# First block of a three-block network: gate and attention output as seven products, with weight sums made by accumulating transfers

## The reference, cut to what matters

```
proj = x @ w_in                       # q, k, v, z_attn, z_ssm, xbc, dt
attn = sliding_window_attention(q, k, v, sinks) * silu(z_attn)
xs, B, C = split(silu(causal_depthwise_conv(xbc)))
y    = ssd_chunked(xs, dt, a, B, C) + xs * d_skip    # 2 chunks of 128, 2 groups of 8 heads
ssm  = gated_rmsnorm(y, z_ssm, ssm_norm_w)           # y * silu(z_ssm), normed per group of 512
out  = concat([attn, ssm]) @ w_out                   # w_out is 2048 x 1024
x    = layer_norm(ALPHA * x + out)
```

## Time and profile before

| | us |
|---|---|
| median of 3 runs | 1921.62 (1921.53 to 1923.89) |
| the profiled execution, its own time | 1921.72 |
| its span | 1919.5 |
| PE busy in the span | 1561.8 (81%) |
| DVE, ACT busy | 681.4 (35%), 306.8 (16%) |

### The profile page before, as it was taken

One profiled execution on the slowest core, in us unless ns is written; L12 is line 12 of the kernel. 1 busy time (PEld: TensorE's weight loads), 2 busy tenths in 40 slices (PEclk: granted clock), 3 DMA queues, 4 the chain that ended last, 5 costly groups with the idle time before them and its releaser, 6 DMA issues.

```text
span 1919.5 us, 20479 instructions
## 1 busy us (share of the span) xinstructions
PE 1561.8 (81%) x8818; PEld 889.4 (46%) x8818; DVE 681.4 (35%) x1395; ACT 306.8 (16%) x806; POOL 16.2 (1%) x45
## 2 busy tenths in 40 slices
PE   9999999999999999675655666555666556899999
PEld 6675477744667845232221222212222122457886
DVE  3663456634486964212110111111111111144533
ACT  1343313442112102000000000000000000213220
POOL 0000000000000000000000000000000000000000
PEclk9999999999999999888887877878787778899999
DMA  9861376523253457999999999999999999954300
GB/s 378 282 174 67 118 271 214 154 102 140 97 175 132 176 220 294 434 431 430 432 431 431 428 432 429 433 429 432 428 432 429 432 430 430 374 186 175 125 8 22
DMA packets 88419, 558.58 MB, mean 291 GB/s; under 512 B 4608, under 2 KB 11552, under 8 KB 74240
## 3 DMA queue, kind: packets, MB, share of 16 engines
q1 hardware_dynamic: 86544, 548.81, 71.3%
...
...
## 4 chain that ended last, share of the span: by engine, by line
PE 58%; DMA 35%; DVE 4%; ACT 1%; issue 1%; POOL 0%; SPq 0%; DVEq 0%; ACTq 0%; POOLq 0%
PE bank L683 26%; DMA ring<-in_w 22%; DMA arena<-in_w 13%; PE bank L1181 8%; PE bank L710 7%; PE bank L692 6%; PE bank L1209 3%; PE bank L671 2%; PE bank L1494 1%; PE bank L885 1%; PE bank L821 1%; PE bank L801 1%; DVE arena L2437 0%; PE bank L1152 0%; PE bank L1232 0%
## 5 line engine op out<-in xcount | busy, mean ns | idle before, releaser
L1181 PE MATMUL bank<-ring,arena 128*32 128x512 f32 x1216 | 288.0, 734 | 148.3 <-DMA arena<-in_w 102.3
L1181 PE MATMUL bank<-arena 128*32 128x512 f32 x832 | 235.5, 733 | 110.6 <-DMA ring<-in_w 98.7
L683 PE MATMUL bank<-ring,arena 128*128 128x512 f32 (+3 forms) x744 | 302.2, 559 | 0.0
L683 PE MATMUL bank<-arena,ring 128*128 128x256 f32 (+1 forms) x1632 | 292.0, 337 | 0.5 <-DVE arena L3116 0.5
L683 PEld LDWEIGHTS bank<-arena,ring 128*128 128x128 f32 x1632 | 256.0, 191 | 31.5 <-issue 7.3
L683 PEld LDWEIGHTS bank<-ring,arena 128*128 128x128 f32 x744 | 138.7, 190 | 134.5 <-issue 123.2
L1181 PEld LDWEIGHTS bank<-ring,arena 128*32 128x32 f32 x1216 | 71.7, 131 | 266.9 <-issue 266.9
L1181 PEld LDWEIGHTS bank<-arena 128*32 128x32 f32 x832 | 57.3, 131 | 202.2 <-issue 202.0
L1209 PE MATMUL bank<-ring,arena 128*32 128x512 f32 x576 | 113.8, 637 | 24.7 <-DMA arena<-in_w 13.8
L710 PE MATMUL bank<-ring,arena 128*128 128x512 f32 (+1 forms) x320 | 127.2, 554 | 2.4 <-DMA ring<-in_w_vd 1.4
L692 PE MATMUL bank<-arena,ring 128*64 128x256 f32 x1024 | 112.6, 380 | 0.0
...
## 6 DMA issues: line engine op xcount, KB each, us to landing
...
ring<-in_w_in SPq DMA_DIRECT2D x40, 2048.0 KB, 8.5
ring<-in_w_mod SPq DMA_DIRECT2D x6, 2048.0 KB, 12.9
ring<-in_w_out SPq DMA_DIRECT2D x6, 2048.0 KB, 8.0
arena<-in_w SPq DMA_DIRECT2D x6, 2048.0 KB, 11.1
ring<-in_w SPq DMA_DIRECT2D x6, 2048.0 KB, 11.7
ring<-in_w_out SPq DMA_DIRECT2D x16, 512.0 KB, 9.6
```

Source lines behind the costliest of these rows:

```text
L683: i = te.matmul(ps, lhsT, rhs, start=n0 + k == 0, stop=n0 + k == n - 1)
L1181: m = te.matmul(ps[32 * j:32 * j + 32, :], LM.xg[:, f, 128 * k + 32 * j:128 * k + 32 * j + 32], vs[j][:, 512 * (k % 2):512 * (k % 2) + 512 ...
```

## The change

Each of the two products is computed by the scheme of Strassen and Winograd: the input is cut in halves of tokens and of channels, the weight in four quadrants, and seven products of 128 tokens x 512 channels x 512 columns (four matmuls each) take the place of eight. The sums that it needs are made in this way.

* Weights: a new input `w_quads` holds the quadrants; SP loads slots `(name, 0)` and `(name, 1)` and a third, `("T", name)`, 2 MB each, for "zs" and "oa". POOL then issues four transfers of 1 MB each that add into their destination (`accum_op=ALU.add`): 1 and 3 add a quadrant from memory, 2 adds one half of T to the other, 4 adds T to the second half of slot 0. So 4 needs 2 and 3 and that product 2 has read slot 0.
* Inputs: four sums of 128x512 on DVE (`layer_token_sums`), for "zs" within the convolution, for "oa" after product 6 of "zs".
* Results: a running sum in `L1.part`; its start is written by ACT, the rest by DVE; tanh now reads `L1.zs`.

In "zs" product 7 comes three turns after product 6, the two between being empty. "oa" goes to the residual `h` at once, and `out_ssm` begins its banks afresh. The gate quarter (1, 0) is made last, after product 7. The turns of ACT's `layer_ssm` are reordered: the squares of a head group come after the first decays of the next. `lng` and `lnb` are loaded at the end of a layer, since the four sums lie in their place. 2 MB slots are counted from 1 instead of 5.

```diff
-            turn, in_turn = [5], list(range(NR))
+            turn, in_turn = [1], list(range(NR))
...
-                for n in range(2):
-                    ns = slice(512 * n, 512 * n + 512)
-                    layer_load(("oa", ly, n), *[(lambda v, a=a, kp=kp: v[64 * a:64 * a + 64, 4 * kp:4 * kp + 4, :],
-                                                 wo[0:1024, ns].rearrange("(k a g d) n -> k a d g n", k=2, a=2, g=4)[kp, a])
-                                                for a in range(2) for kp in range(2)])
+                load_quadrants(("zs", ly, 0), 0, 0)
+                load_quadrants(("zs", ly, 1), 0, 2)
+                load_quadrants(("T", "zs", ly), 0, 2)
+                load_quadrants(("oa", ly, 0), 1, 0)
+                load_quadrants(("T", "oa", ly), 1, 2)
+                load_quadrants(("oa", ly, 1), 1, 2)
...
+            def layer_seven(name, ly, xT):
+
+                w0, w1, T = weights((name, ly, 0)), weights((name, ly, 1)), weights(("T", name, ly))
+                lo, hi = slice(0, 128), slice(128, 256)
+                S = L1.sums
+
+                def times(k, x, w):
+                    ps = fresh("P", name, ly, k, b=4 + ((k - 1) if name == "zs" else k + 6) % 4)
+                    product(ps[:, :], [(x[:, c, :], w[:, c, :]) for c in range(4)]).then_inc(*t.done("mm", "P", name, ly, k))
+                t.wait_ge(*at.of("w", (name, ly, 0)))
+                times(1, xT[:, 0:4, lo], w0[:, 0:4, :])
+                yield
+                times(2, xT[:, 4:8, lo], w0[:, 4:8, :])
+                yield
+                ready(("w", (name, ly, 1)), ("S", name, ly))
+                times(3, S[3], w1[:, 4:8, :])
+                yield
+                ready(("T", name, ly, 1), ("T", name, ly, 2))
+                times(4, S[1], T[:, 4:8, :])
+                yield
+                times(5, S[0], T[:, 0:4, :])
+                yield
+                ready(("T", name, ly, 3))
+                times(6, S[2], w1[:, 0:4, :])
+                t.also("used", (name, ly, 1))
+                yield
+                if name == "zs":
+                    yield
+                    yield
+                ready(("T", name, ly, 4))
+                times(7, xT[:, 4:8, hi], w0[:, 4:8, :])
+                t.also("used", (name, ly, 0))
+                t.also("used", ("T", name, ly))
+                yield
...
-                for g in range(2):
-                    t.wait_ge(*at.of("w", ("zs", ly, g)))
-                    for tt in range(2):
-                        yield from tok512(("zs", ly, tt, g), hT, weights(("zs", ly, g)), tt)
...
                 banks.width = 4
+                yield from layer_seven("zs", ly, hT)
                 ready(*[("ev", "pv", ly, n) for n in range(4)])
...
+                yield from layer_seven("oa", ly, L1.zaT)
...
-                        staged(P[4 + 2 * tt + n][:, :], ("sT", ly), L1.ssmT, weights(("os", ly, n)), tt, 0, 512, 8, 16
-                               ).then_inc(*t.done("mm", "o", ly, tt, n))
+                        staged(fresh("o", ly, tt, n, b=4 + 2 * tt + n)[:, :], ("sT", ly), L1.ssmT, weights(("os", ly, n)),
+                               tt, 0, 512).then_inc(*t.done("mm", "o", ly, tt, n))
...
+                def gate_tanh(tt, g):
+                    to = scratch(("zs", ly, tt, g), 512)
+                    ready(("half", "zs", ly, tt, g))
+                    se.activation(to, L1.zs[:, tt, 512 * g:512 * g + 512], ACT.Tanh).then_inc(*a.done("ev", "zs", ly, tt, g))
+                conv_tanh(CONV[-1])
+                yield
+                ready(("mm", "P", "zs", ly, 1), ("S", "zs", ly))
+                se.mul(L1.part, bank("P", "zs", ly, 1)[:, :], 0.5).then_inc(*a.done("ev", "P", "zs", ly, 1))
+                for gate in (None, None, (0, 0), None, None, (0, 1), (1, 1), None, None):
+                    if gate is not None:
+                        gate_tanh(*gate)
+                    yield
+                ready(("mm", "P", "oa", ly, 1), ("ev", "P", "zs", ly, 7))
+                se.copy(L1.part, bank("P", "oa", ly, 1)[:, :]).then_inc(*a.done("ev", "P", "oa", ly, 1))
+                gate_tanh(1, 0)
...
+                def squares(tt, g):
+                    to, k = scratch(("sq", ly, tt, g), 512), 2 * tt + g
+                    if g == 1:
+                        load_sqrt()
+                    a.wait_ge(*at.of("gated", ly, tt, g))
+                    se.activation(to, L1.y[:, tt, 512 * g:512 * g + 512], ACT.Square,
+                                  accum_out=L1.msum[:, k:k + 1]).then_inc(*a.done("sq", ly, tt, g))
+                    a.also("tmp", "sq", ly, tt, g)
+                    if g == 1:
+                        sqrt(L1.msum[:, 2 * tt:2 * tt + 2], "gn", ly, tt)
...
+                decays(0, 0, 0)
+                yield
+                decays(0, 0, 1)
+                yield
+                yield
+                decays(0, 1, 0)
+                squares(0, 0)
+                yield
+                decays(0, 1, 1)
+                yield
+                decays(1, 0, 0)
+                squares(0, 1)
+                yield
+                yield
+                turned(("sT", ly), L1.ssmT, 0, scale=prm[:, C_N:C_N + 8])
+                yield
+                yield
+                decays(1, 0, 1)
+                yield
+                yield
+                decays(1, 1, 0)
+                squares(1, 0)
+                yield
+                decays(1, 1, 1)
...
+                    if n == 8:
+                        layer_token_sums("zs", ly, hT)
...
+            def layer_token_sums(name, ly, xT):
+
+                lo, hi = slice(0, 128), slice(128, 256)
+                s1, s2, s3, s4 = L1.sums
+                behind()
+                if name == "oa":
+                    ready(("mm", "P", "zs", ly, 6))
+                ve.tensor_tensor(s1, xT[:, 0:4, hi], xT[:, 4:8, hi], ALU.subtract).then_inc(*v.step())
+                ve.tensor_tensor(s3, xT[:, 0:4, lo], xT[:, 0:4, hi], ALU.subtract).then_inc(*v.step())
+                behind()
+                ve.tensor_tensor(s2, s1, xT[:, 0:4, lo], ALU.subtract).then_inc(*v.step())
+                behind()
+                ve.tensor_tensor(s4, xT[:, 4:8, lo], s2, ALU.add).then_inc(*v.done("S", name, ly))
+
...
+                def to_part(dst, k, scale, other, op=ALU.add):
+                    ready(("mm", "P", "zs", ly, k))
+                    behind()
+                    return ve.scalar_tensor_tensor(dst, bank("P", "zs", ly, k)[:, :], scale, other, ALU.mult, op)
+
+                def half(tt, g, k, other, op):
+                    to_part(L1.zs[:, tt, 512 * g:512 * g + 512], k, 0.5, other, op).then_inc(*v.done("ev", "P", "zs", ly, k))
+                    v.also("half", "zs", ly, tt, g)
+
...
+                yield
+                ready(("mm", "sc", ly, 3, 1))
+                to_part(Y, 5, -0.5, X).then_inc(*v.step())
+                half(0, 1, 3, Y, ALU.subtract)
+                gate(0, 0)
+                yield
+                to_part(X, 6, 0.5, X).then_inc(*v.done("ev", "P", "zs", ly, 6))
+                half(1, 1, 5, X, ALU.subtract)
+                yield
+                layer_token_sums("oa", ly, L1.zaT)
+                yield
+                gate(0, 1)
+                yield
+                half(1, 0, 7, X, ALU.add)
+                gate(1, 1)
+                yield
+
...
+                def residual(tt, g, k, other, op):
+                    hv = h[:, tt, 512 * g:512 * g + 512]
+                    behind()
+                    ve.scalar_tensor_tensor(hv, hv, ALPHA, other, ALU.mult, op).then_inc(*v.step())
+                    ready(("mm", "P", "oa", ly, k))
+                    behind()
+                    ve.tensor_tensor(hv, bank("P", "oa", ly, k)[:, :], hv, ALU.add).then_inc(*v.done("ev", "P", "oa", ly, k))
...
-                ve.scalar_tensor_tensor(hv, hv, ALPHA, P[4 + 2 * tt + n][:, :], ALU.mult, ALU.add
-                                        ).then_inc(*v.done("ev", "o", ly, tt, n))
+                ve.tensor_tensor(hv, hv, bank("o", ly, tt, n)[:, :], ALU.add
+                                 ).then_inc(*v.done("ev", "o", ly, tt, n))
...
-                ready(("mm", "k", ly, 0), *([("h", 0, 0), ("h", 0, 1)] if ly else []))
-                ge.dma_start(L1.lng, bcast(ln_g[ly], 1024)).then_inc(*ln.inc())
-                ge.dma_start(L1.lnb, bcast(ln_b[ly], 1024)).then_inc(*ln.inc())
-                at.put(("ln", "loaded", ly), ln.sem, ln.n)
                 ready(("ev", "acsT", ly))
                 ge.dma_start(rows_out[ly].rearrange("t (g n) -> g t n", n=128), L1.Btok[0:16, :].rearrange("g (t n) -> g t n", t=2)
                              ).then_inc(*stored.inc())
                 at.put(("rows", "stored", ly), stored.sem, stored.n)
-                ready(("rows", "stored", ly))
-                for tt, free in enumerate((("mm", "sc", ly, 3, 1), ("mm", "pT", ly, 3, 1, 1))):
-                    ready(free)
+
```

(31 more changed lines are left out.)

130 lines of the change are left out of this document (67 added, 63 removed).

## The result

| | before | after |
|---|---|---|
| median | 1923.15 us (1921.53 to 1923.89, 5 runs) | 1930.78 us (1929.75 to 1932.03, 5 runs) |
| the profiled execution | 1921.72 | 1932.03 |
| its span | 1919.5 | 1930.3 |
| gate to `out_ssm(0)`, layer 0 | 76.47 | 82.28 |
| from there to the same place of layer 1 | 234.73 | 239.96 |

A forecast was written before the change was run, and what follows sets the result against it. PE's columns were taken to set the time, with the ACT, DVE, PE chain right under them. Per layer 6.97 + 1.26 - 3.7 - 2.3 gave about 2.1 us saved, 4.2 for both: 1921.7 - 4.2 = 1917.5 us, range 1912 to 1924.

The forecast's parts named there:

- stall A: Before the first yb of a layer: PE waits for ACT and DVE, 3.7 us of new idle time.
- stall B: Before the transposes sT of chunk 0: the later table load leaves PE idle 2.3 us instead of 0.40.
- nothing in them changes for PE: First yb to second yb: PE's 8.77 us stay as before, so the second yb starts at 182.1.
- sT to yb (1, 0) are 8.07 us without a wait: After the transposes of chunk 0: PE's earlier duration is kept, putting yb (1, 0) at 197.9.
- `out_ssm(0)` needs bank 5 seven us later: After yb (1, 1): the last residual (1, 0) on DVE ends some 0.8 us before bank 5 is needed.
- Rival 2: Small waits on DVE, ACT or bank 5 cost 1 to 2 us a layer, 1919.5 to 1921.5; chance 0.27.
- Within the convolution ... all but 0.1 us: DVE's sums of "zs" delay one convolution by 2.7 us, caught up by the next reciprocal, all but 0.1 us.
- I take 7: Accumulating transfers of 1 MB on POOL's queue: 7 us each to landing, bounded by 4.9 and 12.
- rival 1: Weight sums come late, from 10 us per accumulate on: 1937.4 us at 12 us, 1967 at 15; chance 0.14.
- So hidden: Weight-sum transfers at 7 us each land before the products that need them, so PE doesn't wait.
- Eight matmuls fewer: Between st and the first yb: twelve matmuls become four, removing 6.97 us a layer, 13.9 in all.
- rival 3: The ACT and DVE chain isn't the limit, so each layer saves 6.97 us: 1907.8 us; chance 0.05.

The follow-up runs named there:

- Experiment 1: Changed kernel with unused filler matmuls on PE, four before the first yb and two before the transposes sT of chunk 0, each layer; 1924.27 us.
- Experiment 3: Kernel before the change, with eight unused DVE multiplications ahead of the second M of the first head group in each layer; 1937.21 us.
- Experiment 6: Changed kernel with product 7 of "oa" put in bank 6 instead of bank 5; 1928.95 us.
- Experiment 7: Changed kernel with banks chosen by hand (4 or 3) for three short turns before "st"; 1929.73 us.
- Experiment 4: Changed kernel with its sixteen accumulating transfers replaced by small plain ones, so weights are not summed; 1930.05 us.
- Experiment 11: Changed kernel with squares put back, product 7 in bank 6, sums and tanh moved, three banks, two filler matmuls before yb; 1913.17 us.

## Why the prediction was wrong

* **"3.7 us of idle time is new"** (stall A) and **"2.3 us of idle time where 0.40 was"** (stall B): right, 3.70 and 2.28 us, by the mechanisms given: the four token sums between the two M, and the table load behind the decays.
* **"nothing in them changes for PE"**, said of the stretch from the first yb to the second, and **"sT to yb (1, 0) are 8.07 us without a wait"**: this is the step that failed. It prices an idle spell at its own length and takes the durations behind it from the earlier trace rows, where the longest wait is 0.58 us and the clock 1.00. Behind A, layer 0 lost 1.31 + 2.08 = 3.4 us and layer 1 2.7; behind B 1.7 in each: 9.5 us in the profiled run. Experiments 1 and 3 show it from both sides. That there is such a cost was in reach, its size wasn't: the prediction names both spells, but the earlier trace rows hold none over 0.58 us to read a price from. The Trainium skill, "TensorE: Matmul & The Clock Gate", section "HAM oscillation — how this bites in real kernels", describes a kernel whose waits for transfers put the clock down again and again. The trace agrees that idle time does it, at 0.55 behind 3.70 us.
* **"`out_ssm(0)` needs bank 5 seven us later"**: the bank was looked at for its next user but one. Product 7 needs it first, and waits 1.74 us in each layer. Rival 2 has "the residual misses bank 5", which is this cause, but the sum has it at nothing. Experiment 6 removes it.
* **"Within the convolution ... all but 0.1 us"**: DVE is 0.25 us late at the next reciprocal (137.24 against 136.99) and 0.03 by 144 us, so that holds nearly; but PE comes to "st" 1.71 us late by the four banks, of which the prediction has nothing. With it, yb is at 175.07, not 173.3; that is nearly the whole difference. Experiment 7 takes back half of it in layer 0.
* **"that wait goes"** (0.58 before yb (1, 1)): right.
* **The transfers, "I take 7"**: wrong, 13 us, above the upper bound of 12, and so is the estimate of 6.8 us from the Trainium skill, "DMA: Bandwidth & Descriptors", section "Anatomy of one DMA": here the trace decides. The issues of these transfers took POOL 0.86 to 1.30 us, so none was held for the 2.29 us of rival 1's estimate; **"So hidden"**: right all the same. Rival 1's "from 10 us on" supposed that each holds the queue until it has landed, one after the other; the first three went out within 2.5 us and the fourth could follow 8.3 us after the first, so they overlapped, and its case did not come. Experiment 4 moves the time by no more than the spread.
* **"Eight matmuls fewer"**: right, and the only gain.

Layer 0 was forecast at -2.1 us and came at +5.84, 7.9 apart. The clock gives 5.1, bank 5 1.74, the four banks 1.71: 8.5. Half of the 0.6 too much comes from adding lengths, which overlap: by start times the clock's part is 3.33 from the first yb to the second and 1.43 from sT to yb (1, 0), 4.8 in all. In layer 1 the same terms are 4.4 + 1.74 + 1.71 = 7.9, for 7.3 found. At the medians the miss is 11.8 us, and experiments 1, 6 and 7 take back 6.5, 1.8 and 1.1 of it; what stays is in the banks that experiment 7 leaves and in the spread of the runs.

Rival 2 ("small waits eat it", 1 to 2 us in a layer, +2 to +4) had the right kind of cause and priced it too low: the small waits are 1.74 + 1.71 = 3.45 us in a layer by the trace. No rival had the clock, because a wait was taken to cost nothing beyond itself. Of the signs set down, those on the two waits came true, and those on the length of the stretch, the landing within 10 us and the earlier start of the second block did not. Experiment 11 answers to rival 3: with the chain shortened and PE kept busy, 10.0 of the 13.9 us removed are gained.
